# A product-key expert layer in one fused decoder kernel: tiles 2 to 4 read both expert tables as dense products instead of gathering rows

## The chip, the cores and the metric

The kernel runs on one core of one Trainium2 chip. The metric is the device time of one execution in microseconds; lower is better. Three runs of the kernel before gave 1958.55 to 1961.97 us.

## The reference

One layer of a hybrid decoder for 576 tokens: 64 decode tokens (tile 0) and a prompt of 512 tokens (tiles 1 to 4, 128 each). A token mixer (a state-space scan and window attention, gated and merged) and a layer norm give `x1`. Behind it comes the channel mixer, in which each token chooses, in each of 8 heads, the 16 best of 128 x 128 = 16384 experts. An expert's number is 128 times a first key plus a second key. All in float32:

```python
v1, i1 = lax.top_k(s1, PEER_TOPK)          # s1, s2: (n, 8, 128) key scores
v2, i2 = lax.top_k(s2, PEER_TOPK)
cand = v1[..., :, None] + v2[..., None, :]
cidx = i1[..., :, None] * PEER_KEYS + i2[..., None, :]
sc, sel = lax.top_k(cand.reshape(n, 8, 256), PEER_TOPK)
idx, gate = take_along_axis(cidx, sel), softmax(sc)
h = einsum('nhkd,nd->nhk', peer_u[idx], x1)      # 128 rows of 1024 a token
a = gelu(h) * gate
peer = einsum('nhk,nhkd->nd', a, peer_v[idx])
y = layer_norm(ALPHA * x1 + peer)
```

`peer_u` and `peer_v` have 16384 rows of 1024 floats each, 67.1 MB a table.

## The kernel before, in words

Up to about 290 us the mixer of tiles 0 and 1 runs. From then on the expert layer of the tiles runs in the order 1, 0, 2, 3, 4, and the rest of the mixer, for tiles 2 to 4, is laid between the steps of tiles 1 and 0.

A tile of 128 tokens has 128 slots, one for each of a token's choices (tile 0 folds its 64 tokens into 64 slots of 128 rows). For a slot GpSimd issues two indirect DMAs, `u_row` (L663) and `v_row` (L672), each of which fetches one row of 4 KB for each of the 128 tokens, 0.52 MB. VectorE multiplies the u rows with `x1` and sums (L1462, `do_peer`), ScalarE takes the GELU of four sums (L1762), VectorE multiplies it with the gates (L1431), ScalarE spreads each of these columns on a diagonal (L1754), and TensorE multiplies the diagonal with the v rows into banks 6 and 7 (`weigh`, L1001). Some v rows of tiles 1 and 0 are added on VectorE instead (L1450). The rows land in rings of buffers; GpSimd waits until a buffer has been read. In tiles 2 to 4, ScalarE first copies the tile's `x1` to the first two banks (`do_banks`).

The choice itself is VectorE's work: `top` for each head (L1341 to L1373), `choose` and `index` for each half of the heads, whose lookups compare positions with an iota (L1383 to L1387). The exponentials of the gates are ScalarE's.

The order of all work is one list, written by `schedule()`, that each engine goes through in turn, doing its part of each item. SyncE (SP) loads the weights, 0.5 MB at a time, to the eight slots of `wring` (L584). `do_final` adds the sums to `x1` and does the second layer norm (L1485, L1305); ScalarE then issues the store of the tile (L1776).

## Time and profile before

| | |
|---|---|
| median of 3 runs | 1960.77 us |
| lowest, highest | 1958.55, 1961.97 us |
| profiled execution: span, first to last instruction | 2084.6 us |
| TensorE, VectorE, GpSimd, ScalarE busy in it | 77%, 62%, 59%, 21% |
| DMA: moved, mean rate | 675.08 MB, 324 GB/s |

The profiled execution is another one than the timed three; of it the span is what is known, 123.8 us above the median. Times of rows are microseconds from the start of its span. In a group's row stand the count, the busy time, the mean of one in ns, the idle time of the engine just before, and what ended it. PE is TensorE, PEld its weight loads, DVE VectorE, ACT ScalarE, POOL GpSimd, SP SyncE; PEclk is the share of TensorE's full clock that was granted.

### The profile page before, as it was taken

What the parts mean: (1) busy time and instruction counts of PE and PEld (TensorE: products, weight loads), DVE (VectorE), ACT (ScalarE), POOL (GpSimd) and SP (SyncE); (2) the same over time, 40 slices, a digit from 0 to 9 for tenths busy, and PEclk for the clock granted to TensorE, in tenths of its full rate; (3) what the DMA queues carried; (4) which work ended last, traced back from release to release, by engine and by line L of the source; (5) the groups of instructions that cost most, each with busy time, mean ns of one, the idle gap of its engine ahead of it and who ended that gap; (6) DMA issues with size and microseconds to landing.
All of it is one profiled execution on the core that took longest, in us unless ns stands there. A gap on an engine that the chain in (4) does not pass through costs nothing.

```text
span 2084.6 us, 16770 instructions
## 1 busy us (share of the span) xinstructions
PE 1600.2 (77%) x4829; PEld 811.7 (39%) x4829; DVE 1301.2 (62%) x3093; ACT 442.6 (21%) x1035; POOL 1237.5 (59%) x1370
## 2 busy tenths in 40 slices
PE   7999969798997987974777767577658765777766
PEld 5796655354553432421332323232223322222222
DVE  7820258888888777585786658365758535544345
ACT  2332212354332311111121102111112111111111
POOL 1181027675677657577566667656666675666664
PEclk9999979899998998987888889888888877898987
DMA  6352359997999989899899999989999998999997
GB/s 220 104 156 78 121 209 327 393 342 269 345 405 410 365 329 346 300 351 380 322 342 367 370 371 371 376 313 383 354 368 375 355 393 323 350 369 372 383 377 273
DMA packets 186699, 675.08 MB, mean 324 GB/s; under 512 B 20976, under 2 KB 23456, under 8 KB 186192
## 3 DMA queue, kind: packets, MB, share of 16 engines
q0 software_dynamic: 167056, 609.25, 77.7%
q1 hardware_dynamic: 17632, 59.51, 8.0%
q10 hardware_dynamic: 1920, 5.24, 0.7%
q8 instruction: 40, 0.66, 0.1%
q14 instruction: 51, 0.42, 0.1%
HBM read 669.71 MB, written 3.69 MB: 323 GB/s over the span
## 4 chain that ended last, share of the span: by engine, by line
PE 33%; DVE 20%; POOL 16%; issue 13%; another core or an unknown queue 9%; DMA 7%; ACT 2%; ACTq 0%; POOLq 0%; DVEq 0%; SPq 0%
PE bank L1001 14%; POOL region L672 5%; DVE wring L1462 4%; PE bank L896 4%; POOL region L663 4%; DVE region L1462 4%; POOL wring L663 4%; PE first_banks L896 2%; DMA region<-in_pu,region 2%; DMA wring<-in_pu,region 2%; DMA region<-in_pv,region 2%; PE bank L806 1%; PE bank L713 1%; PE first_banks L806 1%
## 5 line engine op out<-in xcount | busy, mean ns | idle before, releaser
L1001 PE MATMUL bank<-region,small 128*128 128x512 f32 (+1 forms) x1380 | 693.3, 654 | 260.1 <-ACT small L1754 124.0
L672 POOL DMA_INDIRECT region<-in_pv,region x392 | 397.3, 1014 | 250.6 <-issue 104.2
L1001 PEld LDWEIGHTS bank<-region,small 128*128 128x128 f32 (+1 forms) x1380 | 272.4, 204 | 658.2 <-issue 557.8
L663 POOL DMA_INDIRECT region<-in_pu,region x298 | 310.7, 1043 | 194.3 <-issue 84.7
L663 POOL DMA_INDIRECT wring<-in_pu,region x278 | 276.4, 994 | 107.7 <-issue 78.0
L1462 DVE CUSTOM_DVE_ANT_0 wring<-wring,first_banks 128x1024 f32<-128x1024 f32 x228 | 271.7, 1218 | 107.5 <-DMA wring<-in_pu,region 83.0
L1754 ACT ACTIVATE small<-small,region 128x128 f32<-128x128 f32 (+1 forms) x503 | 169.0, 389 | 644.8 <-remote 201.3
L1462 DVE CUSTOM_DVE_ANT_0 region<-region,first_banks 128x1024 f32<-128x1024 f32 x156 | 186.8, 1218 | 72.2 <-DMA region<-in_pu,region 59.9
L1462 DVE CUSTOM_DVE_ANT_0 region<-region 128x1024 f32<-128x1024 f32 x142 | 171.6, 1225 | 38.0 <-DMA region<-in_pu,region 36.5
L1001 PE MATMUL bank<-discretisation,small 128*128 128x512 f32 (+1 forms) x200 | 117.3, 714 | 91.3 <-ACT small L1754 63.3
L1762 ACT ACTIVATE region<-region 128x4 f32<-128x4 f32 x144 | 29.2, 203 | 519.2 <-DVE region L1462 294.6
L1001 PE MATMUL bank<-wring,small 128*128 128x512 f32 x252 | 120.3, 617 | 14.2 <-issue 9.5
L1431 DVE TENSOR_TENSOR region<-region 128x4 f32<-128x4 f32 x144 | 23.1, 161 | 127.6 <-issue 66.1
L1001 PEld LDWEIGHTS bank<-discretisation,small 128*128 128x128 f32 (+1 forms) x200 | 40.2, 213 | 155.0 <-issue 115.8
L1001 PE MATMUL bank<-small 128*128 128x512 f32 (+1 forms) x180 | 93.4, 644 | 7.4 <-issue 6.2
L672 POOL DMA_INDIRECT discretisation<-in_pv,region x60 | 67.1, 1119 | 45.9 <-issue 24.1
L672 POOL DMA_INDIRECT wring<-in_pv,region x64 | 62.2, 971 | 32.6 <-issue 18.8
L1001 PEld LDWEIGHTS bank<-wring,small 128*128 128x128 f32 x252 | 48.4, 197 | 82.4 <-issue 82.0
L1450 DVE SCALAR_TENSOR_TENSOR region<-region 128x1024 f32<-128x1024 f32 x45 | 57.9, 1287 | 33.6 <-issue 25.3
L896 PE MATMUL bank<-xT,wring 128*128 128x192 f32 (+1 forms) x336 | 77.2, 388 | 0.0
L672 POOL DMA_INDIRECT small<-in_pv,region x60 | 61.4, 1023 | 23.2 <-issue 21.8
L1462 DVE CUSTOM_DVE_ANT_0 wring<-wring,region 128x1024 f32<-128x1024 f32 x50 | 60.8, 1222 | 21.3 <-DMA wring<-in_pu,region 20.9
(343 smaller groups left out, 1964.8 us busy)
## 6 DMA issues: line engine op xcount, KB each, us to landing
wring<-in_w SPq DMA_DIRECT2D x100, 512.0 KB, 5.0
region<-in_pv,region POOLq DMA_INDIRECT x392
region<-in_pu,region POOLq DMA_INDIRECT x298
wring<-in_pu,region POOLq DMA_INDIRECT x278
region<-in_w SPq DMA_DIRECT2D x4, 512.0 KB, 6.5
small<-in_small ACTq DMA_DIRECT2D x1, 1669.0 KB, 9.0
xT<-in_xT SPq DMA_DIRECT2D x1, 1536.0 KB, 13.6
region<-in_x SPq DMA_DIRECT2D x3, 512.0 KB
```

The costliest lines, as they stand in the source:

```text
L663: pool.indirect_dma_start(ring_u[u_at.place[q]], None, io["pu"], bass.IndirectOffsetOnAxis(ind[:, k:k + 1], 0)).then_inc(g_u[u_at.place[q] ...
L672: pool.indirect_dma_start(ring_v[v_at.place[q]], None, io["pv"], bass.IndirectOffsetOnAxis(ind[:, k:k + 1], 0)).then_inc(g_v[v_at.place[q] ...
L713: last = mm(b[:, 0:cn], w[:, k, :], xT[:, k, c0:c0 + cn], start=k == 0, stop=k == KT - 1)
L806: last = mm(b[0:tn, 0:n], xT[:, k, t0:t0 + tn], w[:, k % kp, :], start=k == 0, stop=k == KT - 1)
L896: last = mm(b[:, 0:cn], w[:, k0 + k, :], src[:, k, s0:s0 + cn], start=k == 0, stop=k == kn - 1)
L1001: last = mm(bank[6 + hf][0:tn, :], diag[:, d % DIAGS, 0:tn], ring_v[v_at.place[q]][:, 512 * hf:512 * hf + 512], start=k == 0, stop=t > 1 a ...
L1431: V.tensor_tensor(aact[:, n % 2, k], hact[:, n % 2, k], gt[:, k], ALU.mult).then_inc(a_s, 1)
L1450: V.scalar_tensor_tensor(out=acc, in0=ring_v[v_at.place[q]], scalar=aact[:, n % 2, k:k + 1], in1=acc, op0=ALU.mult, op1=ALU.add).then_inc( ...
L1462: V.tensor_tensor_reduce(out=ring_u[u_at.place[q]], in0=ring_u[u_at.place[q]], in1=first_banks[:, :] if t > 1 else x1[t], scale=1.0, scala ...
L1754: S.activation(diag[:, d % DIAGS, 0:tn], eye, ACT.Copy, scale=aact[:, n % 2, k:k + 1]).then_inc(diag_s, 1)
L1762: S.activation(hact[:, n % 2, k], hdot[:, n % 2, k], ACT.Gelu).then_inc(act_s, 1)
```

## The change

Tiles 1 and 0 stay as they are. For tiles 2, 3 and 4 (384 tokens) no row is gathered. Their work is now three passes over chunks of 128 experts, 128 chunks a table; chunk c holds the experts whose first key is c.

- **u pass.** SP streams the u table, 0.52 MB a chunk, through the eight slots of `wring` (`table_chunk`). For each chunk TensorE transposes the 128 x 1024 rows by eight 128 x 128 transposes (`turn_u`), ScalarE copies them to `UT` in two copies of 512 columns, TensorE multiplies them with the transposed `x1` of all 384 tokens (eight matmuls of 384 columns into bank 2), and ScalarE writes the GELU to `hg_block`. Every fourth chunk ScalarE stores the block, 0.79 MB, to `hidden_rows` in HBM. TensorE turns chunk c + 1 ahead of the products of chunk c.
- **gate matrices,** beside the u pass. VectorE does `top`, `choose` and `index` of tiles 2, 3 and 4 at chunks that `TOPS_AT` sets. TensorE transposes first keys, second keys and gates (`turn_choice`). For each token VectorE makes two one-hot matrices of 128 x 128 (slots by keys), one of them times the gates, and one matmul of 128 columns gives the token's gates for all 16384 experts. Four tokens make a group; there are 96, one a chunk from chunk 21, the products three chunks later. ScalarE copies each group to `stage`, and after 16 groups stores the 4.2 MB to `gate_rows` in HBM; before the first copy of the next 16 it waits for that store.
- **v pass.** In blocks of four chunks, SP loads the gates (`gate_in`, rows of 1 KB) and the GELU values (`act_in`, rows of 6 KB), VectorE multiplies them (128 x 1536), and TensorE multiplies with the v table's rows, six matmuls of 512 columns a chunk into six banks. The last eight chunks go tile by tile. Then come the three `do_final`.

The items of tile 2's choice leave the stretch of tiles 1 and 0. Every product stays float32.

```diff
+GATHERED, DENSE = [1, 0], [2, 3, 4]
+CHUNKS = NE // 128
+BLOCK = 4
+CHUNK_SLOTS = 8
+MAJOR = 8
+GATE_TOKENS, HALF = 4, 64
+HALVES = [(t, hf) for t in DENSE for hf in range(2)]
+DTOK = HALF * len(HALVES)
+DENSE_COLS = (TOK - DTOK, TOK)
+GATE_GROUPS = DTOK // GATE_TOKENS
+ONE_HOTS = 4
+TOPS_AT = {2: (0, 1.5), 3: (22, 2.0), 4: (54, 2.0)}
+ONE_HOTS_FROM, GATES_BEHIND = 21, 3
...
-    mix += [[("sc", 2, 0), ("sc", 2, 1)], [("wait",)]] + [[("top", 2, h)] for h in range(2)] + [[("choose", 2, 0)], [("index", 2, 0)]]
...
-                s.append(nxt.pop(0))
-        assert t == 4 or not nxt
-        s.append(("last", t))
-    s.append(("final", ORDER[-1]))
+    s += [("ahead",), ("final", ORDER[1])]
+    at = {c: [] for c in range(CHUNKS)}
+    for t in DENSE:
+        begin, pace = TOPS_AT[t]
+        steps = [[("sc", t, 0), ("top", t, 0)]] + [[("top", t, h)] for h in range(1, 4)] + [[("choose", t, 0)], [("index", t, 0), ("sc", t, 1)]]
+        steps += [[("top", t, h)] for h in range(4, 8)] + [[("choose", t, 1)], [("index", t, 1)]]
+        for n, step in enumerate(steps):
+            at[begin + int(pace * n)] += step
+            if step[0][0] == "choose":
+                at[begin + int(pace * n) + 1].append(("exps", t, step[0][2]))
+        at[begin + int(pace * len(steps)) + 1].append(("turn_choice", t))
+    for j in range(GATE_GROUPS):
+        at[ONE_HOTS_FROM + j].append(("one_hots", j))
+        at[ONE_HOTS_FROM + j + GATES_BEHIND].append(("gates", j))
+    for c in range(CHUNKS):
+        s += [("chunk", c)] + at[c]
+    s += [("sums", b) for b in range(CHUNKS // BLOCK)]
+    s += [("final", t) for t in DENSE]
...
+        UT = view(20224, 2, KT, 128)
+        hg_block = view(28032, 2, BLOCK, DTOK)
+        iota = view(31232, KEYS)
+        choice = view(22272, 2, 3, 128)
+        first_hot = early[:, 0:2048].rearrange("p (a b c) -> p a b c", a=ONE_HOTS, b=GATE_TOKENS)
+        second_hot = view(0, ONE_HOTS, GATE_TOKENS, KEYS)
+        stage = view(5888, KEYS, HALF)
+        gate_in = view(5888, 3, len(HALVES), BLOCK * HALF)
+        act_in = [view(a, BLOCK, DTOK) for a in (10496, 23936, 25472)]
+        hg_rows = nc.dram_tensor("hidden_rows", [CHUNKS // BLOCK, 128, BLOCK * DTOK], F32, kind="Internal").ap()
+        gate_rows = nc.dram_tensor("gate_rows", [len(HALVES), 128, KEYS * HALF], F32, kind="Internal").ap()
...
+            def free_slot(c):
+                if c >= CHUNK_SLOTS:
+                    if c - CHUNK_SLOTS < CHUNKS:
+                        sp.wait_ge(u_turned, 2 * (c - CHUNK_SLOTS) + 2)
+                    else:
+                        sp.wait_ge(v_chunks, c - CHUNK_SLOTS - CHUNKS + 1)
+                elif c < LATER_PIECES:
+                    sp.wait_ge(filled, plan.filled[plan.last_use[holds[c]]])
+                else:
+                    sp.wait_ge(dots, len(on_dve))
+            def table_chunk(c):
+                free_slot(c)
+                table, row = io["pu" if c < CHUNKS else "pv"], 128 * (c % CHUNKS)
+                sp.dma_start(wring[:, c % CHUNK_SLOTS, :], table[row:row + 128, :]).then_inc(chunk_in[c % CHUNK_SLOTS], 16)
+            def block_inputs(b):
+                if b == 0:
+                    sp.wait_ge(gates_out, 16 * len(HALVES))
+                    sp.wait_ge(filled, plan.filled[("sc", DENSE[-1], 1, 1)])
+                if b >= 3:
+                    sp.wait_ge(v_chunks, BLOCK * (b - 2))
+                sp.wait_ge(hg_out[b % 2], 16 * (b // 2 + 1))
+                sp.dma_start(gate_in[:, b % 3], gate_rows.rearrange("h p n -> p h n")[:, :, BLOCK * HALF * b:BLOCK * HALF * (b + 1)]).then_inc(block_in[b % 3], 16)
+                sp.dma_start(act_in[b % 3].rearrange("p a b -> p (a b)"), hg_rows[b]).then_inc(block_in[b % 3], 16)
+            for c in range(CHUNKS):
+                table_chunk(c)
+            block_inputs(0)
+            block_inputs(1)
+            for b in range(CHUNKS // BLOCK):
+                for c in range(BLOCK):
+                    table_chunk(CHUNKS + BLOCK * b + c)
+                if b + 2 < CHUNKS // BLOCK:
...
+            def turn_u(c):
+                pe.wait_ge(chunk_in[c % CHUNK_SLOTS], 16 * (c // CHUNK_SLOTS + 1))
+                if c:
+                    pe.wait_ge(u_columns, 2 * c)
+                for hf in range(2):
+                    for i in range(4):
+                        k = 4 * hf + i
+                        last = tr(bank[hf][:, 128 * i:128 * i + 128], wring[:, c % CHUNK_SLOTS, 128 * k:128 * k + 128], ident)
+                    last.then_inc(u_turned, 1)
...
+            def do_chunk(c):
+                if c + 1 < CHUNKS:
+                    turn_u(c + 1)
+                pe.wait_ge(u_columns, 2 * c + 2)
+                if c:
+                    pe.wait_ge(hidden_act, c)
+                for k in range(KT):
+                    last = mm(bank[2][:, 0:DTOK], UT[:, c % 2, k, :], xT[:, k, DENSE_COLS[0]:DENSE_COLS[1]], start=k == 0, stop=k == KT - 1)
+                last.then_inc(hidden, 1)
...
+            def do_gates(j):
+                if j == 0:
+                    pe.wait_ge(drained["P"], 2 * len(GATHERED))
+                if j >= 2:
+                    pe.wait_ge(staged, j - 1)
+                pe.wait_ge(hots_s, j + 1)
+                for i in range(GATE_TOKENS):
+                    last = mm(bank[6 + j % 2][:, 128 * i:128 * i + 128], second_hot[:, j % ONE_HOTS, i, :], first_hot[:, j % ONE_HOTS, i, :],
+                              start=True, stop=True)
+                last.then_inc(gates_s, 1)
+            def weighted_chunk(v, t):
+                sums, rows = SUM_BANKS[t], act_in[v // BLOCK % 3][:, v % BLOCK, 128 * (t - DENSE[0]):128 * (t - DENSE[0]) + 128]
+                for hf in range(2):
+                    last = mm(bank[sums + hf][:, :], rows, wring[:, v % CHUNK_SLOTS, 512 * hf:512 * hf + 512], start=v == 0, stop=v == CHUNKS - 1)
+                return last
...
+            def do_sums(b):
+                if b == 0:
+                    pe.wait_ge(drained["S"], plan.drained[("sc", DENSE[-1], 1, 1)][1])
+                    pe.wait_ge(staged, GATE_GROUPS)
+                    pe.wait_ge(u_columns, 2 * CHUNKS)
+                first = BLOCK * b
+                if first < CHUNKS - MAJOR:
+                    pe.wait_ge(weighted, b + 1)
+                    for v in range(first, first + BLOCK):
+                        v_here(v)
+                        for t in DENSE:
+                            last = weighted_chunk(v, t)
+                        last.then_inc(v_chunks, 1)
+                elif first == CHUNKS - MAJOR:
+                    pe.wait_ge(weighted, CHUNKS // BLOCK)
+                    for t in DENSE:
+                        for v in range(first, CHUNKS):
+                            if t == DENSE[0]:
...
+            def do_one_hots(j):
+                t, n0 = choice_of(j)
+                dve.wait_ge(choice_s, t - 1)
+                if j == 0:
+                    dve.wait_ge(y_out, 16 * len(GATHERED))
+                if j >= ONE_HOTS:
+                    dve.wait_ge(gates_s, j - ONE_HOTS + 1)
+                for i in range(GATE_TOKENS):
+                    n = n0 + i
+                    V.tensor_scalar(second_hot[:, j % ONE_HOTS, i, :], iota, choice[:, t % 2, 1, n:n + 1], None, ALU.is_equal)
+                    last = V.tensor_scalar(first_hot[:, j % ONE_HOTS, i, :], iota, choice[:, t % 2, 0, n:n + 1], choice[:, t % 2, 2, n:n + 1],
+                                           ALU.is_equal, ALU.mult)
+                last.then_inc(hots_s, 1)
+            def do_sums(b):
+                dve.wait_ge(block_in[b % 3], 32 * (b // 3 + 1))
+                rows = act_in[b % 3].rearrange("p c (h n) -> p c h n", h=len(HALVES))
+                V.tensor_tensor(rows, rows, gate_in[:, b % 3].rearrange("p h (c n) -> p c h n", c=BLOCK), ALU.mult).then_inc(weighted, 1)
...
-                dve.wait_ge(v_used, by_pe[slot_base[t] + n_slots(t) - 1] + (t < 2))
+                tn, sums = TILES[t][1], SUM_BANKS[t] if t in DENSE else 6
+                if t in DENSE:
+                    dve.wait_ge(tile_sums, t - 1)
+                else:
+                    dve.wait_ge(v_used, by_pe[slot_base[t] + n_slots(t) - 1] + 1)
...
+            def columns(c):
+                for hf in range(2):
+                    act.wait_ge(u_turned, 2 * c + hf + 1)
+                    copy(UT[:, c % 2, 4 * hf:4 * hf + 4, :].rearrange("p k n -> p (k n)"), bank[hf]).then_inc(u_columns, 1)
...
+            def do_chunk(c):
+                b = c // BLOCK
+                if c + 1 < CHUNKS:
+                    if c:
+                        act.wait_ge(hidden, c)
+                    columns(c + 1)
+                if c % BLOCK == 0 and b >= 2:
+                    act.wait_ge(hg_out[b % 2], 16 * (b // 2))
+                act.wait_ge(hidden, c + 1)
+                S.activation(hg_block[:, b % 2, c % BLOCK, :], bank[2][:, 0:DTOK], ACT.Gelu).then_inc(hidden_act, 1)
+                if c % BLOCK == BLOCK - 1:
+                    act.wait_ge(hidden_act, c + 1)
+                    act.dma_start(hg_rows[b], hg_block[:, b % 2].rearrange("p a b -> p (a b)")).then_inc(hg_out[b % 2], 16)
...
+            def do_gates(j):
+                per = HALF // GATE_TOKENS
+                h, n0 = j // per, j % per * GATE_TOKENS
+                act.wait_ge(gates_s, j + 1)
+                if h and j % per == 0:
+                    act.wait_ge(gates_out, 16 * h)
+                copy(stage[:, :, n0:n0 + GATE_TOKENS], bank[6 + j % 2].rearrange("p (t a) -> p a t", t=GATE_TOKENS)).then_inc(staged, 1)
+                if j % per == per - 1:
+                    act.wait_ge(staged, j + 1)
+                    act.dma_start(gate_rows[h], stage.rearrange("p a n -> p (a n)")).then_inc(gates_out, 16)
```

TensorE at the end of tile 0, before. `small` holds the diagonals and the key tables, and the rows are one instruction or a run of them:

```order
L1001 MATMUL bank<-discretisation,small 64x512
L1014 MATMUL bank<-region,small 64x512 [waits v_rows_used_by_vector]
L1014 MATMUL bank<-region,small 64x512
L1001 MATMUL bank<-region,small 128x512 [waits diagonal_ready,v_rows_in0,row_sums_read_by_vector]
L1001 MATMUL bank<-region,small 128x512 [waits v_rows_in1,diagonal_ready]
L984 MATMUL bank<-small,region 128x128 [waits scores_read_by_vector,bank_drained_by_scalar]
L984 MATMUL bank<-small,region 128x128 [waits scores_read_by_vector]
```

The same place now:

```order
L1087 MATMUL bank<-region,small 64x512 [waits v_rows_used_by_vector]
L1087 MATMUL bank<-region,small 64x512
L1099 MATMUL first_banks<-small,wring 128x128 [waits scores_read_by_vector,bank_drained_by_scalar,table_chunk_in_slot0,bank_drained_by_vector,bank_filled]
L1099 MATMUL first_banks<-small,wring 128x128 x7
L1099 MATMUL first_banks<-small,wring 128x128 [waits u_columns_ready,table_chunk_in_slot1]
L1099 MATMUL first_banks<-small,wring 128x128 x7
L1113 MATMUL bank<-xT,region 128x384 [waits u_columns_ready]
L1113 MATMUL bank<-xT,region 128x384 x7
L1059 MATMUL bank<-small,region 128x128 [waits scores_read_by_vector,bank_drained_by_scalar]
L1059 MATMUL bank<-small,region 128x128 x3
L1059 MATMUL bank<-small,region 128x128 [waits scores_read_by_vector]
```

The tile 2 products that waited for gathered rows are gone. In their place come the transposes of chunks 0 and 1 (L1099), the products of chunk 0 (L1113), and the key scores of tile 2 (L1059), which stood between row products before.

ScalarE around the first of the six stores of `stage`. `first_banks` is the transposed chunk, `bank` the sums of a chunk or a gate group:

```order
L1966 ACTIVATE region<-bank 128x384 [waits hidden_chunk_summed]
L1969 DMA hidden_rows<-region 128x1536 [waits hidden_chunk_ready]
L1701 ACTIVATE region<-bank 128x128x4 [waits gate_group_summed]
L1987 DMA gate_rows<-region 128x8192 [waits gate_group_staged]
L1701 ACTIVATE region<-first_banks 128x512 [waits u_chunk_transposed,hidden_chunk_summed]
L1701 ACTIVATE region<-first_banks 128x512 [waits u_chunk_transposed]
L1966 ACTIVATE region<-bank 128x384 [waits hidden_chunk_summed,hidden_block_stored0]
L1701 ACTIVATE region<-bank 128x128x4 [waits gate_half_tile_stored,gate_group_summed]
```

One chunk's work (two copies, one GELU) stands between the store's issue and the copy that waits for it, `gate_half_tile_stored`.

SP from its last weights on; L641 are table chunks, L651 and L652 a block's two inputs:

```order
L641 DMA wring<-in_pu 128x1024 [waits bank_filled] x6
L641 DMA wring<-in_pu 128x1024 [waits u_dot_done] x2
L641 DMA wring<-in_pu 128x1024 [waits u_chunk_transposed] x120
L651 DMA region<-gate_rows 128x6x256 [waits hidden_block_stored0,bank_filled,gate_half_tile_stored]
L652 DMA region<-hidden_rows 128x1536
L651 DMA region<-gate_rows 128x6x256 [waits hidden_block_stored1]
L652 DMA region<-hidden_rows 128x1536
L641 DMA wring<-in_pv 128x1024 [waits u_chunk_transposed] x4
```

The u chunks wait for slots; the block inputs 0 and 1 wait for all stores of the gates and stand ahead of the first v chunks.

## Rows read from the trace of the kernel before

**Rows 1.** the page: busy times, slices, queues; GB/s by slice

```profile
PE 1600.2 (77%) x4829; PEld 811.7 (39%) x4829; DVE 1301.2 (62%) x3093; ACT 442.6 (21%) x1035; POOL 1237.5 (59%) x1370
...
GB/s 220 104 156 78 121 209 327 393 342 269 345 405 410 365 329 346 300 351 380 322 342 367 370 371 371 376 313 383 354 368 375 355 393 323 350 369 372 383 377 273
...
q0 software_dynamic: 167056, 609.25, 77.7%
q1 hardware_dynamic: 17632, 59.51, 8.0%
```

**Rows 2.** busy times by stretch (us), then granted clock, DMA share, GB/s

```profile
958.00:2076.00 1118.00, 773.75 (x1604) 317.44 (x1602) 645.75 (x1543) 175.37 (x512) 729.26 (x764) 0.84 0.94 361
1190.00:1200.00 10.00, 10.00 (x25) 4.49 (x24) 9.73 (x20) 1.49 (x5) 7.76 (x8) 1.00 1.01 404
...
72.40:76.20 3.80, 3.80 (x34) 3.56 (x33) 3.49 (x10) 2.76 (x5) 0.00 (x0) 1.00 1.02 401
```

**Rows 3.** timeline of GpSimd near the end: start, duration, idle before

```profile
2049.52 0.94 POOL L672 DMA_INDIRECT region<-in_pv,region  x1 [0.30 <-issue]
...
2059.51 0.94 POOL L672 DMA_INDIRECT wring<-in_pv,region  x1 [0.30 <-issue]
```

**Rows 4.** VectorE, the u dot products: count, duration, first and last start

```profile
L1462 DVE CUSTOM_DVE_ANT_0 region<-region,first_banks x156: 1207/1218/1223, 958.6 to 2060.0; 128x1024 f32<-128x1024 f32 x156
...
L1462 DVE CUSTOM_DVE_ANT_0 wring<-wring,region x50: 1211/1224/1227, 320.9 to 950.1; 128x1024 f32<-128x1024 f32 x50
```

**Rows 5.** timeline of TensorE in the dense mixer work

```profile
569.96 3.60 PE L1001 MATMUL bank<-region,small 128*128 128x512 f32 x8
573.40 5.32 PE L896 MATMUL bank<-xT,wring 128*128 128x384 f32 x16
578.56 3.60 PE L1001 MATMUL bank<-region,small 128*128 128x512 f32 x8
```

**Rows 6.** timeline of TensorE, transposes (L741) and 128-column products (L962)

```profile
72.61 1.91 PE L741 MATMUL bank<-small,region 128*128 128x128 f32 x16
...
262.27 3.84 PE L962 MATMUL bank<-xT,region 128*128 128x128 f32 x32 [0.88 <-ACT xT L1521]
```

**Rows 7.** ScalarE groups by shape: count, busy us, mean ns, idle before

```profile
L1762 ACT ACT_TABLE_LOAD x40 | 51.3, 1283 | 31.7 <-DVE region L1462 31.0
...
L1521 ACT ACTIVATE region<-bank 128x512 f32<-128x512 f32 x19 | 11.3, 593 | 20.1 <-PE bank L741 19.7
...
L1656 ACT ACTIVATE region<-bank,small 128x384 f32<-128x384 f32 x8 | 4.6, 578 | 31.8 <-issue 15.5 <-remote 11.7 <-PE bank L896 4.5
L1521 ACT ACTIVATE hgT<-bank 128x288 f32<-128x288 f32 x6 | 4.1, 691 | 0.2
```

**Rows 8.** VectorE: two groups by shape, then first and last of one top-16

```profile
L1193 DVE TENSOR_SCALAR stat<-stat 128x4 f32<-128x4 f32 x9 | 1.6, 173 | 0.3
...
L1441 DVE TENSOR_SCALAR region<-region 128x1024 f32<-128x1024 f32 x1 | 0.7, 693 | 2.3 <-DMA small<-in_pv,region 2.3
...
1225.80 0.49 DVE L1341 MAX8 region<-bank 128x8 f32<-128x128 f32 x2
...
1231.19 0.42 DVE L1373 FIND_INDEX8 region<-region 128x8 uint32<-128x256 f32 x1
```

**Rows 9.** DMA issues: KB each, us to landing

```profile
small<-in_small ACTq DMA_DIRECT2D x1, 1669.0 KB, 9.0
```

**Rows 10.** timeline from the end of tile 0 into tile 2

```profile
957.77 1.93 PE L1014 MATMUL bank<-region,small 128*64 128x512 f32 x4 [0.64 <-DVE region L1450]
...
970.01 0.51 ACTq L1776 DMA_DIRECT2D out_y<-region  x1
...
971.88 6.38 PE L1001 MATMUL bank<-region,small 128*128 128x512 f32 x8 [12.18 <-ACT small L1754]
```

**Rows 11.** timeline of the last microseconds

```profile
2075.40 1.41 DVE L1483 TENSOR_TENSOR region<-region,bank 128x512 f32<-128x512 f32 x2
...
2082.19 0.34 ACTq L1780 DMA_DIRECT2D out_y<-region  x1
```

159 lines of the change are left out of this document (87 added, 72 removed).

## The prediction

> **What bounds the kernel now.** The page's first parts come first [rows 1]: TensorE is busy 77% of the span and GpSimd 59%, and from the seventh slice on the DMA engines move 270 to 410 GB/s in every slice. A mean over the span says little here, so the busy times by stretch come next [rows 2]. From 958 to 2076 us, where tiles 2 to 4 gather, TensorE works 774 of 1118 us at 0.84 of its clock, GpSimd 729 us, and the DMA share is 0.94 at 361 GB/s. The dot products mark this stretch: those of tiles 2 to 4 start at 958.6 and end at 2060 [rows 4].
>
> Two limits lie close together there. Tiles 2 to 4 have 384 slots of two gathers, 768 in all. On GpSimd each takes 0.94 us and 0.30 us of issue, 1.25 us from start to start [rows 3], which makes 960 us. The gathers move 768 x 0.524 = 403 MB; at the 404 GB/s of the best 10 us [rows 2] that is 997 us. The stretch takes 1118. So the gathers are the bound, by descriptors and bytes alike, and arithmetic waits for them. Only something that reads fewer bytes, and not from GpSimd, helps here. The change reads each table once: 134 MB, with 50 MB written and 50 MB read back for its own two intermediates, 235 MB instead of 403.
>
> **The change part by part,** on the scale of the profiled execution.
>
> *Up to the end of tile 0:* 960 us. Its last product ends at 957.8 + 1.9 [rows 10]. The choice of tile 2 leaves this stretch, but the gathers that bound it stay. I take no gain, and hold 10 us either way possible.
>
> *The turn:* 7 us. ScalarE's first GELU of a chunk stands behind the store of tile 0. Before, that store was issued at 970.0 and took 0.5 us to issue [rows 10], with four dot products ahead of the final that are gone; 970.5 - 960 less 4 us is about 7. The first u chunks load meanwhile.
>
> *The u pass:* TensorE's rates at full clock come from the dense mixer work. Eight products of 512 columns lie 3.44 us before the next group, 0.43 us each, and sixteen of 384 columns 5.16 us, 0.3225 us each [rows 5]. Transposes and products of 128 columns run at 0.12 us each [rows 6]. A chunk is 8 x 0.12 + 8 x 0.3225 = 3.54 us, 128 chunks 453 us. A group of four gate products is 0.48 us, 96 groups 46 us. Together **499 us**, if TensorE never waits.
>
> A rule of the Trainium skill speaks against this (TensorE: Matmul & The Clock Gate, Part 4: PE-mode transpose): a 128 x 128 transpose measured about 275 ns in a kernel, and transposes don't count as work that lifts the clock. At 0.275 us each the sum would be 128 x 8 x 0.155 = 159 us more, an estimate by that page of 2002 us in place of the forecast. The trace has thirty-two in 3.8 us at a granted clock of 1.00 [rows 2, 6], so the sum keeps 0.12.
>
> What waits are added to the 499? First, **ScalarE stops at five of the six stores of the gates,** since one chunk after the issue it needs the buffer back. A transfer of 4.19 MB is not in the trace. The nearest, 1669 KB, lands in 9.0 us [rows 9]: by its rate 22.6 us, by the best DMA rate 10.4 us. I take 15, since chunk loads are few here. TensorE can go on for two chunks, 8 us, then idles 7. After an idle time of 12.18 us eight products took 6.38 us in place of 3.60 [rows 5, 10], 2.8 us for the clock. With 1 us for ScalarE to catch up each store costs 11 us, five cost 55; bounds 10 and 100. Second, the exponentials of a half tile need two table loads of 1.28 us [rows 7]. ScalarE's work in a chunk is two copies of 0.6 us, a GELU near the 0.58 us of 384 columns, and the copy of a gate group of 0.6 to 1.2 us, 2.4 to 3.0 us of 4.02; most of the loads disappears in the rest. I take 10 us for six; bounds 0 and 20. Third, **VectorE.** A top-16 takes 5.8 us [rows 8] and stands at every second chunk in two stretches of 25 chunks, beside 16 one-hot instructions. These are not in the trace; a tensor-scalar of 1024 columns takes 0.69 us and one of 4 columns 0.17 [rows 8], which makes 0.24 us for 128; independent ones start before the last has ended, and I take 0.2 us (bounds 0.13 and 0.3). Two chunks then ask 9.0 us of VectorE and 8.04 of TensorE, 24 us in all; the store waits give some of it back, and I take 10; bounds 0 and 60. The u pass is 574 us. Its loads, 0.52 MB in 4 us, ask 131 GB/s, nothing against 361.
>
> *The v pass:* 128 x 6 x 0.43 = **330 us** on TensorE, a block of four chunks 10.3 us. Its DMAs bring 2.10 + 0.79 + 0.79 = 3.67 MB: 9.1 us at 404 GB/s, 10.2 at 361. Hardware-queue transfers here, 59.5 MB for 8.0% of sixteen engines, moved 357 GB/s [rows 1]. The two limits are again close. The gates come in rows of 1 KB, a kind that has no row of its own; bounds 9.1 us and, if they go at a quarter of the rate, 16 us a block. I take 10.6 us, **340 us.** Loads are issued eight chunks and two blocks ahead, so VectorE's multiplication (1536 columns; 1.22 us for 1024, [rows 4]) is hidden; without that lead it would add its 1.8 us to each block, 58 us.
>
> *The end:* 9 us. The final of tile 4 has the steps of before, 2075.4 to 2084.6 [rows 11]; those of tiles 2 and 3 are hidden behind the tile-wise last products, 6.9 us each.
>
> Sum: 960 + 7 + 574 + 340 + 9 = **1890 us**, against the profiled 2084.6. The median of the runs is 123.8 us below that span. I lay this on the gathers, which filled 1789 us, because the rest is short; the changed kernel gathers for 675 us and keeps 47 us of it. That gives **1843 us,** 6% less than 1960.77. If instead all work stretched alike under the profiler, it would be 1890 x 0.9406 = 1778.
>
> **The rivals.**
>
> *The v pass is bound by its DMAs, and the kernel is slower.* Place: the two inputs of a block, queued ahead of v chunks. Price: the change loses once the pass takes 330 + 10 + 118 = 458 us, 14.3 us a block, 257 GB/s. For it: 1 KB rows never seen here, and 1669 KB alone came at 185 GB/s [rows 9]. Against: 345 to 410 GB/s in the slices [rows 1]. At 240 GB/s: 1843 + 149 = 1992 us. Chance 0.10.
>
> *ScalarE or VectorE sets the pace of the u pass.* The copy of a gate group reads and writes with strides; a strided copy of 288 columns took 0.69 us [rows 7], 2.4 ns a column, 1.2 us for 512, and with both sides strided perhaps twice that. ScalarE would then need 4.2 us and its waits between, some 4.8 us a chunk instead of 4.02. With one-hots at 0.25 us VectorE needs the same. 96 x 0.8 is 77 us: 1920 us. Chance 0.20; still faster.
>
> *Better than forecast.* Stores at 10 us, VectorE in step, the v pass at 330 us, and part of the profiler's stretch off TensorE's work: 1843 - 45 - 10 - 10 - 10 = 1768 us. Chance 0.20.
>
> *The clock stays at its lower level (1.2 GHz) in the u pass.* A mechanism of this kernel: a quarter of each chunk is transposes, and every store leaves an idle time. The u pass would take up to 499 us more, 2342 us. The rule on transposes above would have it so; the granted clock of 1.00 among transposes [rows 2] speaks against it. Chance 0.03.
>
> That the gathers don't go isn't one: the instruction order shows 384 indirect DMAs left of 1152.
>
> **How the numbers follow.** Forecast 1843 (1800 to 1890) 0.47, the rivals 0.10, 0.20, 0.20, 0.03. The range of 8 in 10 takes the better case in and goes up over the pace rival to where the DMA rival starts: 1755 to 1965. A measurement of this kernel can tell 0.2%, 4 us, from no change. Faster holds the forecast, the better case and most of the pace rival, 0.84; same 0.02; slower the DMA and clock rivals and the pace rival's far end, 0.14.
>
> **What would show it.** Right: GpSimd idle after 960 us; chunks of 3.5 us, 4.0 with gates; five gaps of TensorE of about 7 us, 16 chunks apart, ended by ScalarE behind the gate store; 10.3 to 10.6 us a block in the v pass with the DMA share above 0.9; clock near 1.00 but after the gaps. Wrong: a steady wait for the GELU or the copies in each chunk; a gap of VectorE's making at `turn_choice` or the gates; v blocks over 12 us with TensorE waiting for table chunks or weighted blocks; any stretch of the u pass at the lower clock.

## The result and the profile after

The changed kernel takes **2516.8 us** (median of four, 2515.5 to 2518.7) beside 1959.7 us before: a ratio of 1.285, 95% interval 1.283 to 1.287. The measured time lies far outside the forecast of 1843 us and its range (1755 to 1965), and the sign is wrong: 28% slower instead of 6% faster.

The page of the changed kernel; its rows answer to [rows 1]:

```profile
span 2514.1 us, 23966 instructions
...
PE 2358.3 (94%) x8666; PEld 1384.1 (55%) x8666; DVE 1072.5 (43%) x3004; ACT 531.0 (21%) x1020; POOL 487.4 (19%) x602
...
PE   8999798898898879999999999999999999999998
...
PEclk9989899899899899999999999999999999999999
DMA  5532499979999993332424243443444444444442
GB/s 208 138 116 101 174 370 387 327 291 387 372 388 392 360 354 114 109 121 96 165 101 159 101 159 132 141 167 101 184 168 175 175 177 181 182 182 183 182 184 75
...
PE 77%; DMA 8%; DVE 6%; POOL 5%; issue 3%; ACT 2%; SPq 0%; ACTq 0%; DVEq 0%; POOLq 0%
```

From the sixteenth slice on TensorE is full at full clock, and the DMA engines, nearly full in the nine slices before, run at 96 to 184 GB/s up to the last. The last line, the shares of the chain that ended last, is three quarters TensorE. The change did what it says: GpSimd is idle behind 955 us, and the kernel moves 508 MB in place of 675. So the bytes were saved, and TensorE took their place as the bound.

Its groups, by line and shape (count, busy us, mean ns, idle before):

```profile
L1113 PE MATMUL bank<-xT,region 128*128 128x384 f32 x2048 | 689.9, 491 | 2.3 <-ACT region L1966 2.3
L1141 PE MATMUL bank<-wring,region 128*128 128x512 f32 x1024 | 459.2, 592 | 0.0
...
L1141 PE MATMUL first_banks<-wring,region 128*128 128x512 f32 x512 | 239.4, 592 | 0.0
...
L1099 PE MATMUL first_banks<-small,wring 128*128 128x128 f32 x1024 | 134.4, 275 | 17.1 <-ACT region L1701 17.1
...
L1133 PE MATMUL bank<-hgT,region 128*128 128x128 f32 x768 | 101.5, 275 | 0.0
```

The counts are the answer. A record here is one instruction in the trace. The u pass has 128 chunks x 8 products = 1024 in the source, and the trace has 2048. The v pass has 128 x 6 = 768 and the trace 1536. The gates have 384 and the trace 768. The transposes have 1024 and the trace 1024. **A float32 product is two instructions, a transpose one.** One chunk of the u pass and a piece of the v pass on the timeline (start, us, idle before in brackets) show the durations:

```profile
1300.95 1.05 PE L1133 MATMUL bank<-hgT,region 128*128 128x128 f32 x8
...
1301.85 1.04 PE L1099 MATMUL first_banks<-small,wring 128*128 128x128 f32 x8
...
1302.72 5.33 PE L1113 MATMUL bank<-xT,region 128*128 128x384 f32 x16
...
1307.88 1.05 PE L1133 MATMUL bank<-hgT,region 128*128 128x128 f32 x8
1308.14 0.49 ACT L1966 ACTIVATE region<-bank 128x384 f32<-128x384 f32 x1 [4.51 <-PE bank L1113]
```

```profile
2303.78 3.60 PE L1141 MATMUL bank<-wring,region 128*128 128x512 f32 x8
...
2305.72 1.76 DVE L1653 TENSOR_TENSOR region<-region 128x1536 f32<-128x1536 f32 x1 [19.13 <-DMA region<-hidden_rows]
...
2307.21 1.88 PE L1141 MATMUL first_banks<-wring,region 128*128 128x512 f32 x4
```

A chunk with gates is 6.93 us: 16 instructions from 1302.72 to 1307.88, 0.3225 us each. That is exactly the 0.3225 of [rows 5], but there are twice as many as the source has products. ScalarE's GELU waits 4.5 us for them and VectorE waits 19 us in a block, while TensorE waits for another engine only 19 us in the whole u pass (17.1 and 2.3 in the rows above). The eight v instructions start 3.43 us before the next group, 0.43 us each, but they are four products. An instruction's time goes with its columns: 0.11 us for 128 (eight gate instructions in 0.90 us), 0.3225 for 384, 0.43 for 512. So the streaming of columns sets it and not the load of the 128 x 128 weights, which is the same in all three.

### The profile page after: what moved, and what is told of

Read it like the earlier page. It is cut to its first block, busy times and chain, and to the rows that moved or that the text cites. A ratio compares the mean times of both kernels' runs of the same rounds, so it can differ in the third digit from the quotient of the medians.

```text
span 2514.1 us, 23966 instructions
## 1 busy us (share of the span) xinstructions
PE 2358.3 (94%) x8666; PEld 1384.1 (55%) x8666; DVE 1072.5 (43%) x3004; ACT 531.0 (21%) x1020; POOL 487.4 (19%) x602
## 3 DMA queue, kind: packets, MB, share of 16 engines
q0 software_dynamic: 56464, 206.55, 22.1%
## 4 chain that ended last, share of the span: by engine, by line
PE 77%; DMA 8%; DVE 6%; POOL 5%; issue 3%; ACT 2%; SPq 0%; ACTq 0%; DVEq 0%; POOLq 0%
PE bank L1113 25%; PE bank L1141 17%; PE first_banks L1141 9%; PE first_banks L1099 4%; PE bank L1076 3%; PE bank L1133 3%; DMA gate_rows<-region 3%; PE bank L971 3%; DMA region<-in_pu,region 2%; PE first_banks L971 2%; POOL region L747 2%; POOL region L738 2%; DMA region<-in_pv,region 2%; DVE region L1616 1%; PE bank L788 1%
## 5 line engine op out<-in xcount | busy, mean ns | idle before, releaser
L1113 PE MATMUL bank<-xT,region 128*128 128x384 f32 x2048 | 689.9, 491 | 2.3 <-ACT region L1966 2.3
L1113 PEld LDWEIGHTS bank<-xT,region 128*128 128x128 f32 x2048 | 382.5, 192 | 245.0 <-issue 10.0
L1141 PE MATMUL bank<-wring,region 128*128 128x512 f32 x1024 | 459.2, 592 | 0.0
L1141 PEld LDWEIGHTS bank<-wring,region 128*128 128x128 f32 x1024 | 194.6, 190 | 244.7 <-issue 244.4
L1141 PE MATMUL first_banks<-wring,region 128*128 128x512 f32 x512 | 239.4, 592 | 0.0
L1076 PE MATMUL bank<-region,small 128*128 128x512 f32 (+1 forms) x352 | 171.6, 630 | 26.3 <-DMA region<-in_pv,region 16.3
L738 POOL DMA_INDIRECT region<-in_pu,region x142 | 161.5, 1137 | 112.1 <-DVE region L1464 44.2
L747 POOL DMA_INDIRECT region<-in_pv,region x136 | 149.0, 1096 | 82.2 <-PE bank L1076 45.0
L1701 ACT ACTIVATE region<-first_banks 128x512 f32<-128x512 f32 (+2 forms) x281 | 151.4, 586 | 36.1 <-PE first_banks L1099 17.7
L1099 PE MATMUL first_banks<-small,wring 128*128 128x128 f32 x1024 | 134.4, 275 | 17.1 <-ACT region L1701 17.1
L1099 PEld LDWEIGHTS first_banks<-small,wring 128*128 128x128 f32 x1024 | 117.4, 142 | 27.5 <-issue 23.7
L1076 PEld LDWEIGHTS bank<-region,small 128*128 128x128 f32 (+1 forms) x352 | 63.1, 186 | 118.0 <-issue 99.2
L1701 ACT ACTIVATE region<-bank 128x512 f32<-128x512 f32 (+7 forms) x156 | 86.9, 559 | 129.3 <-DMA gate_rows<-region 43.8
## 6 DMA issues: line engine op xcount, KB each, us to landing
gate_rows<-region ACTq DMA_DIRECT2D x6, 4096.0 KB, 14.3
```

The costliest lines, as they stand in the source:

```text
L738: pool.indirect_dma_start(ring_u[u_at.place[q]], None, io["pu"], bass.IndirectOffsetOnAxis(ind[:, k:k + 1], 0)).then_inc(g_u[u_at.place[q] ...
L747: pool.indirect_dma_start(ring_v[v_at.place[q]], None, io["pv"], bass.IndirectOffsetOnAxis(ind[:, k:k + 1], 0)).then_inc(g_v[v_at.place[q] ...
L1076: last = mm(bank[6 + hf][0:tn, :], diag[:, d % DIAGS, 0:tn], ring_v[v_at.place[q]][:, 512 * hf:512 * hf + 512], start=k == 0, stop=False)
L1099: last = tr(bank[hf][:, 128 * i:128 * i + 128], wring[:, c % CHUNK_SLOTS, 128 * k:128 * k + 128], ident)
L1113: last = mm(bank[2][:, 0:DTOK], UT[:, c % 2, k, :], xT[:, k, DENSE_COLS[0]:DENSE_COLS[1]], start=k == 0, stop=k == KT - 1)
L1141: last = mm(bank[sums + hf][:, :], rows, wring[:, v % CHUNK_SLOTS, 512 * hf:512 * hf + 512], start=v == 0, stop=v == CHUNKS - 1)
```

## The experiments

Theory A: TensorE bounds both passes because each float32 product costs two instructions of the length I had read. Rival B: a product is one instruction's time, and another engine or a wait paces the u pass. Rival C: the transfers pace the v pass. The lines of code below are those of the changed kernel. In all half precision runs x, the table chunks or the other operands named are rounded to float16 before TensorE; the sums stay float32. Runs without a range were executed once, and their differences are taken from the changed kernel's profiled execution (2515.9 us).

**1. Half of the u products.**

```diff
-                for k in range(KT):
-                    last = mm(bank[2][:, 0:DTOK], UT[:, c % 2, k, :], xT[:, k, DENSE_COLS[0]:DENSE_COLS[1]], start=k == 0, stop=k == KT - 1)
+                for k in range(KT // 2):
+                    last = mm(bank[2][:, 0:DTOK], UT[:, c % 2, k, :], xT[:, k, DENSE_COLS[0]:DENSE_COLS[1]], start=k == 0, stop=k == KT // 2 - 1)
```

> The changed kernel with four of the eight products of each u chunk, so that every hidden value is summed over half of its 1024 terms; transposes, copies, loads and waits stay. Theory A (TensorE bounds the u pass and each float32 product is two instructions of 0.3225 us): 512 products fewer at 0.645 us, 330 us less, about 2187 us. Rival B (a product is one instruction's time, and ScalarE, VectorE or the DMA pace the pass): 512 x 0.3225 us = 165 us less at most, about 2352 us, and nothing at all if another engine paces it. Theory A allows less than 330 us where ScalarE's two copies, GELU and gate copy (2.3 us a chunk) and the turns between the engines become the limit: a chunk would be 3.54 us plus 1.0 for the gates.

Measured: 2225.8 us, 290 us less (330 expected by A, 165 at most by B). The u products end at 1554.6 us in place of 1845.1, and the v pass keeps its 660 us. 290 is 88% of 330 and 1.8 times B's bound. A chunk with gates takes 4.35 us, TensorE's own work still: 2.58 us from the first product to the gates, 0.89 and 0.87 us for gates and transposes.

```profile
1265.45 1.04 PE L1099 MATMUL first_banks<-small,wring 128*128 128x128 f32 x8
1266.32 2.75 PE L1113 MATMUL bank<-xT,region 128*128 128x384 f32 x8
1268.90 1.05 PE L1133 MATMUL bank<-hgT,region 128*128 128x128 f32 x8
1269.79 1.04 PE L1099 MATMUL first_banks<-small,wring 128*128 128x128 f32 x8
```

What is missing from the 330 lies in the waits for the gate stores, which the shorter chunks no longer cover:

```profile
L1113 PE MATMUL bank<-xT,region 128*128 128x384 f32 x1024 | 358.0, 493 | 3.7 <-ACT region L1966 3.7
...
L1099 PE MATMUL first_banks<-small,wring 128*128 128x128 f32 x1024 | 137.9, 279 | 46.7 <-ACT region L1701 46.7
```

TensorE waits 46.7 us for ScalarE's copies where the changed kernel had 17.1: 30 of the missing 40 us. Another 7 lie ahead of the pass, where the gathers of tiles 1 and 0 ended later: the first u product starts at 954.7 us in place of 947.6.

**2. A third of the v products,** for rival C.

```diff
-                        for t in DENSE:
+                        for t in DENSE[:3 if v == 0 else 1]:
```

> The changed kernel with the v chunks before the last eight multiplied for one of the three tiles alone (the other two tiles keep chunk 0's block of columns and the last eight chunks, so their sums lack most rows). All loads stay. Theory A: 2 products instead of 6 a chunk, 1.7 us at 0.86 us each, which is under the time of a chunk's transfers; the v pass falls from 660 us to what the DMA engines need for 64 MB of table and 50 MB of hidden and gate rows, 290 to 340 us, and the kernel to 2150 to 2200 us. Rival C (1 KB runs of the gate rows make the DMA engines pace the v pass already): it stays near 660 us and the kernel near 2510 us. Rival B (6 products are 2.6 us, the rest of the 5.15 us a chunk is waiting for something else): it falls by 1.7 us a chunk or less, about 2310 us or more.

Measured: 2189.8 us, 326 us less. The stretches (PE, PEld, DVE, ACT, POOL busy, then granted clock, DMA share, GB/s):

```profile
955.00:1845.00 890.00, 871.46 (x3888) 593.60 (x3887) 353.83 (x1446) 262.39 (x494) 0.00 (x0) 0.99 0.39 136
1845.00:2100.00 255.00, 208.04 (x427) 86.15 (x426) 43.95 (x25) 1.98 (x3) 0.00 (x0) 0.91 0.96 363
```

The u pass is untouched; the v pass, with its loads unchanged, runs at a DMA share of 0.96. Its first 120 chunks take 292 us: from the first v product at 1845.2 to the end of the last at 2178.7, less 48 products of 0.86 us for the last eight chunks. That is 2.43 us a chunk, 9.7 a block; the changed kernel takes 20.6 a block. So rival C falls, and with it the fear that the gates' rows of 1 KB would set the pace of the float32 kernel.

**3. The u products in half precision.** Same counts of products, copies and bytes; ScalarE writes the turned chunk as float16.

```diff
-        UT = view(20224, 2, KT, 128)
+        UT = view(20224, 1024).bitcast(F16).rearrange("p (a k n) -> p a k n", a=2, k=KT)
+        xh = [view(21248, 960).bitcast(F16).rearrange("p (k n) -> p k n", k=5), view(14336, 576).bitcast(F16).rearrange("p (k n) -> p k n", k=3)]
...
-                    last = mm(bank[2][:, 0:DTOK], UT[:, c % 2, k, :], xT[:, k, DENSE_COLS[0]:DENSE_COLS[1]], start=k == 0, stop=k == KT - 1)
+                    last = mm(bank[2][:, 0:DTOK], UT[:, c % 2, k, :], xh[k // 5][:, k % 5, :], start=k == 0, stop=k == KT - 1)
```

> The changed kernel with the u products in half precision: ScalarE writes the turned chunk as float16, and the 384 tokens' x is copied once as float16; counts of products, copies, transfers and waits stay, and the hidden values are rounded. Theory A (float32 products are taken in two passes of half speed): in one pass at full speed a product of 384 columns takes 0.16 us, so 1024 of them fall from 660 us to 164 us, and the u pass goes from about 890 us to about 400 us, where ScalarE's copies (2.3 to 2.9 us a chunk) pace it; the kernel comes to 2010 to 2080 us. Rival B (what TensorE is given does not matter, others pace the u pass): within 50 us of 2516 us. The TensorE records of that line should fall from 2048 to 1024.

Measured: 2118.7 us, 397 us less. B falls: apart from two copies that round x once, only the type of TensorE's operands had changed. The group and one chunk of it:

```profile
L1117 PE MATMUL bank<-region 128*128 128x384 f16 x1024 | 196.6, 337 | 3.3 <-ACT region L1973 3.3
```

```profile
1258.67 1.09 ACT L1705 ACTIVATE region<-first_banks 128x512 f16<-128x512 f32 x2
...
1258.85 1.46 PE L1117 MATMUL bank<-region 128*128 128x384 f16 x8
```

1024 products are 1024 instructions, and eight lie in 1.46 us, of which the last shows 0.33: 0.161 us each, a quarter of 0.645. So 384 columns cost 1.0 cycle each of the 2.4 GHz clock in float16 and 4.0 in float32. The time missed its forecast of 2010 to 2080 us by 39, on the slow side. Most chunks with gates now take 3.06 us, and that is still TensorE's own work (0.87 + 0.90 + 1.29), not ScalarE's copies. The mean of the pass is 3.7 us because TensorE stops: it idles 63.9 us for ScalarE, mostly in the gate stores, which now stop it for up to 12 us each, and 14.4 us for VectorE's one-hots. These 78 us are most of the 115 us that the pass takes above 32 x 2.16 + 96 x 3.06 = 363 us. VectorE is 91% busy from 1000 to 1100 us.

**4. The v products in half precision** (ScalarE copies each v chunk as float16, VectorE writes gate times hidden as float16, a chunk's slot comes free with ScalarE's copy, and the last eight chunks go chunk by chunk like the others).

> The changed kernel with the v pass alone in half precision: ScalarE copies each v chunk as float16 (128 copies of 128x1024, about 1.1 us each, beside the products), VectorE writes gate times hidden as float16, TensorE multiplies these; u pass and gates stay float32, and the weighted rows are rounded. Theory A: six products of 512 columns in one pass take 1.3 us instead of 5.15 us a chunk, so the transfers pace the pass at about 2.4 us a chunk, as where two thirds of the products were left out (2190 us in all): 2160 to 2200 us. If the DMA had room for more than that run showed, or if the copies on ScalarE stood in the way, it would fall outside: 2.9 us a chunk or more would be 2230 us and up. Rival B and rival C: near 2516 us.

Measured: 2190.4 us, as predicted. This run and those of experiments 5 to 7 fell on another chip than experiments 1 to 3. There the changed kernel takes 2529.4 us (experiment 8), so the change saves 339 us. All six products a chunk are there, and the v products take 305 us (1862.2 to 2167.6) in place of 659: the transfers pace the pass.

```profile
L1144 PE MATMUL bank<-region 128*128 128x512 f16 x512 | 160.4, 444 | 97.0 <-ACT region L1706 97.0
...
L1706 ACT ACTIVATE region<-wring 128x1024 f16<-128x1024 f32 x128 | 134.9, 1056 | 168.7 <-DMA wring<-in_pv 166.3 <-PE first_banks L1144 1.8 <-ACT region L1971 0.5
```

TensorE waits for ScalarE's copy, and the copy waits 166 us for the chunk to land.

**5. Both, and the one-hots of the gates too.**

> The u pass, the v pass and the one-hots of the gate products all in float16 (the x of the 384 tokens, the turned chunks, the hidden values times gates, the gate factors and the v rows are rounded). In the run with the u pass alone in half precision a chunk took 3.8 us, VectorE was busy 91% of 1000 to 1100 us and TensorE 84%: the gates and the one-hots pace it. Theory A: 2119 us less 340 for the v pass, and less 48 us where gate products (two passes of 0.12 us) were on the path; VectorE's one-hots may be shorter in half precision or not. 1700 to 1790 us. If float32's two passes were not the whole of the u and v passes' length, the two savings would not add up, and it would stay above 1850 us.

Measured: 1740.2 us, inside the 1700 to 1790 expected. The savings nearly add up: 2190.4 less the 397 of experiment 3 is 1793. A group of four gate products adds 0.23 us to a chunk (2.40 us in place of 2.17) where it added 0.90 in float32, a quarter again; 96 x 0.67 = 64 us would bring the kernel to 1729. The 11 us above that fit VectorE's one-hots, for which TensorE now waits 33.2 us in place of 14.4. The dense form is now faster than the kernel before, which takes 2079 us on this chip; in float32 it had lost by 28%.

**6. Gates and hidden values as float16 in DRAM, two staging buffers.** Both take half the room, so blocks of eight chunks keep the 1 KB runs. Only the gate copy is shown of the edit:

```diff
-                if h and j % per == 0:
-                    act.wait_ge(gates_out, 16 * h)
-                copy(stage[:, :, n0:n0 + GATE_TOKENS], bank[6 + j % 2].rearrange("p (t a) -> p a t", t=GATE_TOKENS)).then_inc(staged, 1)
+                if h > 1 and j % per == 0:
+                    act.wait_ge(gates_out, 16 * (h - 1))
+                copy(stage[:, h % 2, :, n0:n0 + GATE_TOKENS], bank[6 + j % 2].rearrange("p (t a) -> p a t", t=GATE_TOKENS)).then_inc(staged, 1)
```

> As the one with all in half precision, and the gates and hidden values are also stored in DRAM and read back as float16, with blocks of eight chunks (so the runs of the gate rows are again 1 KB) and two staging buffers for the gates. It takes away the wait for a half tile's gates to be stored (64 us in five waits with the u pass in half precision) and half of the 50 MB that is read back, a fifth of the v pass's traffic. Expected: 40 to 60 us less in the u pass, and in the v pass 20% of about 320 us less, so 1600 to 1680 us. If the gate stores only hid behind VectorE's work, 1660 to 1720 us.

Measured: 1629.2 us (four executions). The first v product starts at 1382.0 us in place of 1422.7, 41 less, and the v products take 230.8 us (1382.0 to 1612.8) in place of 294.7, 64 less: both terms as expected. The v pass is at the DMA engines' limit. The u pass is at VectorE's only where the choices of tiles 3 and 4 stand beside the one-hots, as in the first row; 55 of its 96 chunks with gates take 2.40 us, TensorE's own 0.87 + 1.29 + 0.23.

```profile
1100.00:1200.00 100.00, 76.86 (x587) 56.88 (x585) 95.99 (x413) 62.19 (x118) 0.00 (x0) 0.96 0.63 220
...
1500.00:1600.00 100.00, 83.68 (x342) 34.56 (x341) 10.55 (x6) 62.23 (x59) 0.00 (x0) 0.91 1.04 402
```

**7. Half of the one-hots on GpSimd,** idle behind the gathers; else as 6, which ran again beside it.

```diff
-                    V.tensor_scalar(second_hot[:, j % ONE_HOTS, i, :], iota, choice[:, t % 2, 1, n:n + 1], None, ALU.is_equal)
...
+                    last = pool.tensor_scalar(second_hot[:, j % ONE_HOTS, i, :], iota, choice[:, t % 2, 1, n0 + i:n0 + i + 1], None, ALU.is_equal)
```

> As the run above, with half of the one-hots (128x128, one per token, 384 of them) made by GpSimd, which was idle behind the gathers. In that kernel VectorE was busy 91 to 96% of 1000 to 1300 us and its one-hots are 0.45 us a pair. If VectorE paces the u pass there, 384 x 0.2 = 77 us of its work go, and the pass gets 40 to 75 us shorter until ScalarE and TensorE pace it (about 3.0 us a chunk): 1550 to 1590 us. If the turn between TensorE and ScalarE sets the 3.1 us a chunk anyway, or GpSimd needs over 0.75 us for one, it stays at 1620 to 1640 us or gets longer.

> The kernel with all in half precision and float16 rows again (1629 us on a chip on which the kernel before took 2079 us), for its ratio on this chip. On a chip where the kernel before takes 1957 us: 1590 to 1630 us, a ratio of 0.81 to 0.83; on one like the last, 0.78 again.

Measured: **1587.3 us** with GpSimd (1585.7 to 1594.0) and 1623.1 without (1621.8 to 1625.1). The first v product starts at 1339.5 us, 39 before the 1378.1 of the run beside it. Of these, 6 lie ahead of the u pass (first u product at 959.1 in place of 965.1) and 33 in it, where the chunks beside the choices (24 to 80) take 187 us in place of 220. So VectorE did pace that part of the pass. The 33 us are less than the 40 to 75 expected; the sum came inside its range of 1550 to 1590 by help of the 6. GpSimd needs 0.60 us for most one-hots, 0.66 in the mean:

```profile
L772 POOL TENSOR_SCALAR region<-region 128x128 f16<-128x128 f32 x384 | 247.6, 662 | 120.0 <-ACT region L1720 82.2 <-PE bank L1152 37.5
```

Against the kernel before on the same chip, 2079 us, the ratio of the kernel with GpSimd is 0.764 (95% interval 0.761 to 0.767), and that of experiment 6, run beside it, 0.780 (0.777 to 0.782); its first runs had given 0.784.

**8. The profiled execution of before, again,** and the changed kernel once more, both without an edit. The first profile of before lay 124 us above its median, and 47 us of the forecast hung on why.

> The kernel before, profiled once more. In the first trace of it the span was 2084.6 us and the time of that execution 2084.6 us, 123.8 us over the median of its runs, while the changed kernel's profiled execution lies within 2 us of its median. If the excess belongs to the gathers of tiles 2 to 4 of that one execution, as the forecast assumed, a second profile either shows it again in the same place (the rows on GpSimd and the DMA queues between 960 and 2075 us) or is near 1960 us with tile 0 still ending near 960 us. If profiling itself costs 124 us, it comes back at about 2085 us with the excess spread over the whole span.

> The kernel before, profiled a third time, on whichever chip the call falls. So far: 2084.6 us in the first profile (360 GB/s between 1340 and 1700 us), 1957.4 us in the second (408 GB/s), and seven unprofiled executions of 2065 to 2084 us on the chip of the last call. If the gathers' rate depends on the chip, this one is either near 1957 us with the DMA share above 1.0 in all of 1000 to 1900 us, or near 2075 us with dips to 350 GB/s there, and the runs beside it say the same; if it varies from one execution to the next, the profile and the runs beside it differ.

> The changed kernel once more, on the same chip as the run above. Theory A: TensorE bounds both passes with the DMA engines at 35 to 50%, so the chip's DMA rate does not matter and it takes 2510 to 2520 us again, wherever the kernel before takes 1957 or 2075 us. Were the v pass bound by transfers (rival C), it would move with the kernel before, by up to 40 us.

Measured: 1959.2 us in one profile, 2074.5 us in a later one on the other chip, each like the unprofiled runs beside it (1956.5, and 2065 to 2089). The gathers of tiles 2 and 3 in the two profiles, first the 1959 us one:

```profile
1340.00:1700.00 360.00, 272.74 (x549) 103.58 (x548) 235.44 (x557) 61.53 (x187) 263.11 (x276) 0.93 1.03 408
```

```profile
1340.00:1700.00 360.00, 251.60 (x536) 105.64 (x537) 212.43 (x521) 56.03 (x169) 235.40 (x247) 0.84 0.95 360
```

The second is the first profile [rows 2: 0.94 and 361 GB/s] over again. So the excess belongs to the gathers on one chip (or to something it shared there), not to profiling. And it belongs almost wholly to those of tiles 2 to 4: the last product of tile 0 ends at 952.5 us in the fast profile and at 958.0 and 959.7 in the two slow ones. The changed kernel took 2529.4 us on that chip, 13 us more: chunk 0's transposes start at 956.7 us in place of 944.7, the v products at 1858.9 in place of 1845.4. So 12 of the 13 us lie where tiles 1 and 0 gather, and both passes kept their lengths. Why the gathers run 12% slower there, while the streamed tables of experiment 6 reach 402 GB/s on the same chip, was not tried and stays open.

## Why the prediction was wrong

**The step that failed** is the first of the u pass: "Eight products of 512 columns lie 3.44 us before the next group, 0.43 us each, and sixteen of 384 columns 5.16 us, 0.3225 us each." The rows hold eight and sixteen *instructions*. I multiplied their time by the products counted in the source, so every product came at half its price: 330 of the 453 us of the u pass, the 46 us of the gates and the 330 us of the v pass. Only the transposes were priced right. The mechanism of the forecast, TensorE as the bound of the u pass, was right; the price of a product was not. It is 0.645 us for 384 columns and 0.86 us for 512, twice what I took. The sum, term by term:

| term | forecast | measured |
|---|---|---|
| first u product behind tile 0 | 967 | 947.6 |
| transposes, u products, gates | 499 | 859 (32 chunks of 6.07, 96 of 6.93) |
| waits and the rest of the u pass | 75 | 39 |
| v pass | 340 | 659 (1536 x 0.429) |
| end | 9 | 9 |
| between profile and median | -47 | +3 |
| sum | 1843 | 2517 |

With 0.645 and 0.86 us a product the forecast's own terms give 128 x (8 x 0.12 + 8 x 0.645) = 783, 384 x 0.24 = 92 and 768 x 0.86 = 660, in all 960 + 7 + 875 + 75 + 660 + 9 = 2586 on the profiled scale, slower than before by a wide margin.

Of the signs set down beforehand, GpSimd's idleness and the clock came true. The chunks failed theirs, 6.07 and 6.93 us in place of 3.5 and 4.0, and so did the v pass, 20.6 us a block in place of 10.3 to 10.6 at a DMA share of 0.45 in place of above 0.9. Of the signs of being wrong only one half came, v blocks over 12 us, and without its other half, TensorE waiting. The signs looked for waits and for the lower clock, and a doubled price of TensorE's own work makes neither.

The trace of before could have told it. The products of `do_wq` for tiles 2 to 4, one loop of eight heads by eight k of 128x384, are 64 in the source. Its records there:

```profile
L953 PE MATMUL first_banks<-xT,wring x112: 326/486/634, 298.6 to 902.0; 128*128 128x384 f32 x64, 128*128 128x192 f32 x48
...
L953 PE MATMUL bank<-xT,wring x112: 326/486/590, 302.7 to 896.8; 128*128 128x384 f32 x64, 128*128 128x192 f32 x48
```

64 and 64 are 128. The Trainium skill says the same from another side (FP8 and Floating Point Precision, section TensorE Precision Notes): true FP32 takes four passes through the array, while float16 and bfloat16 are raised to the native precision and multiplied there. The trace agrees in the price, four cycles a column, and shows it as two instructions of two cycles a column each; that each of them holds two of the four passes is a reading that no run here shows. A float32 transpose, one instruction, costs two cycles a column as well (0.11 us for 128).

**The limits of the forecast, point by point.**

- *The gathers bound the kernel before.* Right, and more so than I said: on the faster chip the DMA share is 1.02 or 1.03 and the rate 406 to 410 GB/s in every stretch from 958 to 1900 us.
- *The clock in the u pass* and the 0.12 us a transpose: right. The granted clock is 0.99, and eight transposes and eight gate instructions lie 0.87 and 0.90 us from start to start of the next group. The rule of the Trainium skill by which a transpose takes 0.275 us (TensorE: Matmul & The Clock Gate, Part 4: PE-mode transpose) agrees with the mean of 275 ns in the rows, but that is how long one lasts and not how far apart they start, and a sum needs the 0.11 us between starts. Whether transposes count for the clock, the other half of that rule, this loop can't tell, because 5.16 us of products lie between them.
- *The gate stores.* A store of 4.19 MB lands in 14.3 us (15 taken). ScalarE waits 43.8 us in five, but TensorE only 16, for a chunk of 6.9 us covers more than the 4.0 I had reckoned with. With chunks of 3.06 us (experiment 3) TensorE loses 63.9 us; my 55 belongs to that case. A slip in the bound: 1669 KB here are 1.709 MB, 190 GB/s and not 185, so the slow bound for a store is 22.1 us and not 22.6.
- *VectorE.* One-hots come at 0.225 us (0.2 taken). It was no limit at 6.9 us a chunk, cost TensorE 14.4 us of waits in experiment 3 and 33.2 in experiment 5, and paced the chunks beside the choices in experiment 6.
- *ScalarE's strided copy* of a gate group: 0.60 us, like any other of 512 columns. The pace rival falls.
- *The v pass at its DMA limit:* 9.7 us a block in experiment 2, in the middle of the 9.1 to 10.2 forecast; the changed kernel, at 20.6 us a block, never reached the limit.
- *The turn* of 7 us wasn't there: TensorE starts chunk 0's products at 947.6, before tile 0 is stored at 951.2. Most of the other 12 us between 967 and 947.6 come from the chip: the first profile of before looks like the slow one's, and on that chip the changed kernel's tile 0 ends 12 us later. The key scores of tiles 2 to 4, 10.3 us of TensorE, I had left out.
- *The 47 us:* the size was wrong, and so was the key by which I shared out the 124 us. They are the chip's and not the profiler's, but 120 of the 127 us between the first profile and the fast one lie behind the end of tile 0, in gathers that the change removes. The changed kernel differs by 13 us between the chips. This was a second, smaller error, and it made the forecast lower as well, by some 35 us.

None of the rivals was that TensorE bounds both passes at twice my price, and the range left no room for it.

## What to carry to other kernels

Before a duration from a trace is multiplied by a count from the source, count one known loop in the trace: 64 products there may be 128 records. In float32, bytes saved by dense products are paid on TensorE at four cycles a column; here about 330 us of gathers a tile gave way to some 520 us a tile of products. In float16 the v pass of the same dense form is bound by its transfers, and with the gates and hidden values stored in float16 and GpSimd's help the kernel took 0.76 of the time of before on the second chip, if the rounding is allowed.

## What the runs showed that was not expected

The first is that the gather kernel's time differed by 6% between the two chips (1957 and 2079 us) while dense streaming hardly did: the v pass at its DMA limit moved 363 GB/s on the first (experiment 2) and 374 on the second (experiment 4, 1870 to 2160 us). The second is that TensorE rows overlap: the mean of 491 ns (u products) stands beside a spacing of 322.5 ns, so a group's mean times its count (1006 us) is far from its length, and its busy time (690 us for 660 us of spacing at full clock) comes nearer. The third is that a float16 result costs ScalarE no less: 128x512 to float16 takes 602 ns in experiment 6, to float32 595 in the changed kernel. VectorE too writes a float16 one-hot in the time of a float32 one (295 and 281 ns).
